# Two products instead of three for every split projection, with ScalarE making the first parts of 30 weights

## The chip, the cores and the metric

The kernel runs on one core of a Trainium2 chip. The metric is the device time of one execution in microseconds (us), lower is better. TensorE multiplies; VectorE, ScalarE and GpSimd work on tiles of 128 partitions; SyncE issues the transfers.

## The reference

Two transformer blocks in float32 on 512 tokens of width 1024 (the second has 16 more tokens of its own, 528 in all), and every matrix product is wanted to float32's accuracy:

```python
# block 1
proj = rms_norm(x, pre_gain) @ w_in              # q, k, v, z_a, b, c, u, z_c
attn = rms_norm(diff_attention(q, k, v)) * silu(z_a)
x = x + rms_norm(concat(attn, conv) @ w_out)     # wo
e = rms_norm(p @ w_ple_proj)
x = x + sigmoid(x @ w_ple_gate) * e              # pg
# block 2
n = rmsnorm(h) @ w_in_2                          # c_q, c_kv, k_pe, gq, gk, gv, gg, gates
y_a = mla_branch(...); y_b = gla_branch(...)
mix = sigmoid(gate_a) * (y_a @ w_o_mla) + sigmoid(gate_b) * (y_b @ w_o_gla)   # ta, oa, tb, ob
h = h + mix @ w_out_2                            # w2
h = h + peer_ffn(rmsnorm(h), w_q, sub_keys, u_tab, v_tab)     # pq, ps, top-k, experts
```

## The kernel before

**Split projections.** A float32 matrix is held as two float32r matrices that TensorE multiplies at its fast rate: a first part, rounded, and the rest. Weights come in groups of 1 MB (128 partitions x 8 x 256 float32), each with a name: q0, k0, v0, q1, ... for block 1, `wo0` to `wo3` for its output projection, `pg0` to `pg3` for its gate; in block 2 cq, ckv, kpe, gq, gk, gv, `ta`, `gg0` to `gg3` (gate of GLA), `tb0` to `tb3` and `ob0` to `ob3` (second gate and output), `w20` to `w23` (output projection), `pq0` to `pq7` (queries of the experts' part, one for each head). `SPLIT` is the list of the split ones in TensorE's order. A weight group is 16 tile products of 512 columns (for the weights that stand as the moving matrix, 32 of 256; in the second block's first projections, 512 tokens and the 16 more go as pieces of 264). `three()` (L799) issues three matmuls for each: first x first (L802), first x rest (L803), rest x first (L804).

**Who makes the parts.** SyncE brings weights into `wring`, NW = 4 slots. On GpSimd `split_group(i)` (L2562) waits for the transfer and, as there are only NU = 2 part buffers, for TensorE's last job with the weights two before (`when_filled(pool, last_job(SPLIT[i - NU]))`), then makes the first part (4 casts of 128x512, L2577) and the rest (4 subtractions, L2581), and signals `weights_split`, for which TensorE waits in `split_arrived` (L792). ScalarE makes first parts of weights only for q0 and k0 (L1516, L1522) and, in `query(h)`, pq6 and pq7 (L1852). For activations, ScalarE rounds (round_gained L1505, round_h L1528, round_pair L1562) and VectorE subtracts (`lower` L2010, L1984, split_pair L2061).

**The stages** in TensorE's order, in us of the profiled execution: block 1's projections and attention 0 to 227; `wo` 227 to 278.5; the gate `pg` to 347.5, whose results pass for each of four m through ScalarE (sigmoid), VectorE (product, sum, gain) and ScalarE (square, rounding); block 2's norm and first projections to 396; MLA's; MLA attention and further projections to 676; GLA to 846; gates and outputs `gg`, `tb`, `ob`, and `w2` to 1028; `pq0`, `pq1` to 1055; the heads' top-k with `pq2` to `pq7` in between to 1137. Then the experts' part: each tile of the table u is multiplied in two products (L1386, L1387) to 1650, and the weighted sum over v (L1438, L1439) to the end. That part already holds its matrices by another rule: with SCALE = 128, GAIN = 127/128, the first part is the rounding of GAIN times the matrix and two products suffice.

**Order.** Each engine works its own list in order; semaphores (`fills`, `empties`, `when_filled`) hand tiles over. In the top-k stretch VectorE picks 16 best for each of 8 heads, GpSimd weighs places (L2613) between its weights, and TensorE scores keys (ps) from `pq`.

## Time and profile before

| | us |
|---|---|
| median of 3 runs | 2176.15 |
| lowest, highest | 2173.21, 2176.32 |
| span of the profiled execution | 2175.9 |
| TensorE busy | 2115.4 (97%) |
| VectorE busy | 1304.1 (60%) |
| GpSimd busy | 1033.5 (47%) |
| ScalarE busy | 922.6 (42%) |

Times of an execution are read from the start of its span. The profiled execution lies within the range of the runs. A row of a timeline gives start, length, engine, line, operation, tiles written and read with shape, how many in a row (x4), and in brackets how long the engine had been idle before it and which instruction ended that. A row of a window gives the stretch, its length, and for each engine its busy time and number of instructions. "PEclk" is the share of full clock that TensorE was granted. Busy times of matmuls overlap, so a row's mean is longer than the distance of two matmuls.

### The profile page before, as it was taken

The page shows a single profiled execution, that of the slowest core. Times are in us where ns is not written, and L with a number is a line of the kernel's source. Part 1 is how long each engine was busy: PE and PEld are TensorE (multiplying, and loading weights), DVE is VectorE, ACT ScalarE, POOL GpSimd, SP SyncE. Part 2 cuts the span into 40 slices and gives each one's busy share as a digit, 9 for nine tenths or more (in the row PEclk, how much of TensorE's full clock was granted, in tenths as well). Part 3 has the DMA queues.
Part 4 walks back from the last instruction along what each step waited for, and adds up shares of the span by engine and source line. Part 5 has one row for each costly group of instructions (what it writes and reads, how often), then busy time and mean ns, then how long its engine had stood idle before and what let it go on. Part 6 is the DMA issues. An engine that isn't in the chain of part 4 may idle for free.

```text
span 2175.9 us, 27394 instructions
## 1 busy us (share of the span) xinstructions
PE 2115.4 (97%) x10296; PEld 1661.6 (76%) x10296; DVE 1304.1 (60%) x2244; ACT 922.6 (42%) x1528; POOL 1033.5 (47%) x892
## 2 busy tenths in 40 slices
PE   8999999999999999999999998999999899999999
PEld 6877767557887776887878877777778788888887
DVE  6456257352235774215898957888881666666664
ACT  4223343572234234111334447777773434343432
POOL 6655546212324122877859887999996100000000
PEclk9999999999999999999999999999999999999999
DMA  5222312201111111233216664777788988888884
GB/s 201 100 78 78 116 61 90 90 30 49 59 40 59 59 55 43 97 122 110 78 59 199 205 206 141 272 289 246 272 291 294 333 300 286 289 284 300 288 287 149
DMA packets 98291, 359.32 MB, mean 165 GB/s; under 512 B 8480, under 2 KB 41504, under 8 KB 73328
## 3 DMA queue, kind: packets, MB, share of 16 engines
q1 hardware_dynamic: 98160, 357.56, 47.3%
q8 instruction: 83, 1.36, 0.3%
q14 instruction: 48, 0.39, 0.1%
HBM read 286.09 MB, written 71.30 MB: 164 GB/s over the span
## 4 chain that ended last, share of the span: by engine, by line
PE 67%; POOL 13%; DVE 11%; issue 6%; ACT 2%; DMA 1%; POOLq 0%; SPq 0%; ACTq 0%; DVEq 0%
PE ps L1438 11%; PE ps L1439 11%; PE ps L802 10%; PE ps L803 9%; PE ps L804 9%; POOL area L2643 6%; POOL wring_parts L2621 6%; PE ps L791 2%; PE ps L1249 2%; DVE area L2413 2%; PE ps L1386 1%; PE ps L1387 1%; DVE area L2410 1%; PE ps L884 1%; PE ps L1225 1%
## 5 line engine op out<-in xcount | busy, mean ns | idle before, releaser
L2577 POOL CAST wring_parts<-wring 128x512 fp32r<-128x512 f32 x236 | 170.5, 764 | 546.0 <-PE ps L804 429.3
L1386 PE MATMUL ps<-sqbuf_parts,wring_parts 128*128 128x512 f32 x1024 | 412.6, 403 | 5.5 <-POOL wring_parts L2621 5.5
L1387 PE MATMUL ps<-normed_x_parts,wring_parts 128*128 128x512 f32 x1024 | 404.4, 395 | 0.0
L2621 POOL TENSOR_TENSOR wring_parts<-wring_parts,wring 128x512 fp32r<-128x512 f32 x256 | 331.0, 1323 | 76.0 <-ACT wring_parts L1856 73.0
L2581 POOL TENSOR_TENSOR wring_parts<-wring,wring_parts 128x512 fp32r<-128x512 f32 x244 | 351.2, 1470 | 6.6 <-ACT wring_parts L1852 1.5
L1386 PEld LDWEIGHTS ps<-sqbuf_parts,wring_parts 128*128 128x128 f32 x1024 | 194.0, 189 | 50.6 <-POOL wring_parts L2621 4.9
L1387 PEld LDWEIGHTS ps<-normed_x_parts,wring_parts 128*128 128x128 f32 x1024 | 193.9, 189 | 41.8
L802 PE MATMUL ps<-resid_parts,wring_parts 128*128 128x512 f32 (+1 forms) x528 | 201.2, 381 | 6.1 <-DVE normed_x_parts L2010 3.3
L803 PE MATMUL ps<-normed_x_parts,wring_parts 128*128 128x512 f32 (+1 forms) x528 | 197.0, 373 | 0.0
L804 PE MATMUL ps<-resid_parts,wring_parts 128*128 128x512 f32 (+1 forms) x528 | 196.2, 372 | 0.0
L1474 ACT ACTIVATE area<-ps 128x1024 f32<-128x1024 f32 (+6 forms) x89 | 61.7, 696 | 275.2 <-PE ps L804 183.5
L2504 DVE COPY area<-ps 128x512 f32<-128x512 f32 x128 | 138.9, 1087 | 56.3 <-PE ps L1413 56.3
L803 PE MATMUL ps<-area_parts,wring_parts 128*128 128x512 f32 x440 | 172.4, 392 | 0.0
L1888 ACT ACTIVATE area<-area,rt 128x128 bf16<-128x128 bf16 x512 | 156.5, 390 | 3.7 <-DVE area L2494 3.7
L1878 ACT ACTIVATE area<-ps 128x512 f32<-128x512 f32 x128 | 76.3, 597 | 187.0 <-PE ps L1387 187.0
L802 PE MATMUL ps<-area_parts,wring_parts 128*128 128x512 f32 x376 | 150.1, 399 | 4.8 <-POOL wring_parts L2581 2.3
L804 PE MATMUL ps<-area_parts,wring_parts 128*128 128x512 f32 x376 | 146.7, 390 | 0.0
L1438 PE MATMUL ps<-cst_parts,area_parts 128*128 128x512 f32 x352 | 138.3, 393 | 4.7 <-issue 4.7
L1439 PE MATMUL ps<-rt_parts,area_parts 128*128 128x512 f32 x352 | 138.0, 392 | 0.0
L1856 ACT ACTIVATE wring_parts<-wring 128x1024 fp32r<-128x1024 f32 x128 | 134.4, 1052 | 7.2 <-DMA wring<-in_uT_dram 7.2
L1438 PE MATMUL ps<-normed_x_parts,area_parts 128*128 128x512 f32 x352 | 136.9, 389 | 0.0
L1439 PE MATMUL ps<-normed_x_parts,area_parts 128*128 128x512 f32 x352 | 136.9, 389 | 0.0
(269 smaller groups left out, 4431.4 us busy)
## 6 DMA issues: line engine op xcount, KB each, us to landing
wring<-in_weights_dram SPq DMA_DIRECT2D x65, 1024.0 KB, 4.8
wring<-in_uT_dram SPq DMA_DIRECT2D x128, 512.0 KB, 4.4
area<-in_vT_dram SPq DMA_DIRECT2D x44, 1024.0 KB, 7.2
hidden_table<-area SPq DMA_DIRECT2D x32, 1024.0 KB, 6.7
gate_table<-area SPq DMA_DIRECT2D x32, 1024.0 KB, 8.4
area<-gate_table SPq DMA_DIRECT2D x32, 1024.0 KB, 9.1
wring<-in_vT_dram SPq DMA_DIRECT2D x20, 1024.0 KB, 6.7
rt<-hidden_table SPq DMA_DIRECT2D x32, 512.0 KB, 4.6
```

The costliest lines, as they stand in the source:

```text
L802: pe.matmul(out, a_up, b_up, start=first, stop=False)
L803: pe.matmul(out, a_up, b_low, start=False, stop=False)
L804: return pe.matmul(out, a_low, b_up, start=False, stop=last)
L1386: pe.matmul(out, first[:, d], h_first[:, k, :], start=(k == 0), stop=False)
L1387: mm = pe.matmul(out, rest[:, d], h_rest[:, k, :], start=False, stop=(k == KD - 1))
L1438: pe.matmul(out, v_first[:, j, d], c_first[:, t], start=(n == 0 and j == 0), stop=False)
L1439: mm = pe.matmul(out, v_rest[:, j, d], c_rest[:, t], start=False, stop=(n == HALVES - 1 and j == 1))
L1888: ins = act.activation(gateB[:, q, i, 0, :], oneB[:, q, i, :], ACT.Copy, scale=entT[:, 2, t:t + 1])
L2504: dve.tensor_copy(dst[:, 4 * i:4 * i + 4, :], spread_out(n)).then_inc(copied, 1)
L2577: ins = nc.gpsimd.tensor_copy(up[:, d, :], W(name)[:, d, :])
L2581: ins = nc.gpsimd.tensor_tensor(low[:, d, :], W(name)[:, d, :], up[:, d, :], ALU.subtract)
L2621: ins = nc.gpsimd.tensor_tensor(rest[:, a:a + PIECE], first[:, a:a + PIECE], u_raw[t % len(USLOT)][:, a:a + PIECE], ALU.subtract)
```

## The change

`three()` becomes `two()`: the first part is now the rounding of GAIN times the weight (or 1/SCALE times the activation), the rest is the first part minus the weight (or 127 times the first part minus the activation), and out = (first x first + rest x rest) comes out 1/128 of the product. The factor 128 is folded into what reads the result. Three gain vectors are multiplied by 128 once at the start, and two additions of VectorE become scalar_tensor_tensor. For 30 weights, listed in `AHEAD_W`, ScalarE makes the first part in two halves of 1024 elements (`round_ahead`), and GpSimd starts its first two subtractions after the first half and the others after the second. All other weights stay on GpSimd, whose cast becomes a multiplication with GAIN.

```diff
+AHEAD_W = ([f"wo{m}" for m in (2, 3)] + [f"pg{m}" for m in range(4)] + ["cq0", "cq1", "gg2", "gg3", "tb0", "ob0", "tb1", "ob1"]
+           + ["tb2", "ob2", "tb3", "ob3"] + [f"w2{m}" for m in range(4)] + [f"pq{m}" for m in range(HP)])
...
-            def three(out, a_parts, b_parts, first, last):
-
-                (a_up, a_low), (b_up, b_low) = a_parts, b_parts
-                pe.matmul(out, a_up, b_up, start=first, stop=False)
-                pe.matmul(out, a_up, b_low, start=False, stop=False)
-                return pe.matmul(out, a_low, b_up, start=False, stop=last)
+            def two(out, a_parts, b_parts, first, last):
+
+                (a_first, a_rest), (b_first, b_rest) = a_parts, b_parts
+                pe.matmul(out, a_first, b_first, start=first, stop=False)
+                return pe.matmul(out, a_rest, b_rest, start=False, stop=last)
...
+            def round_ahead(name):
+
+                i = SPLIT.index(name)
+                up, _ = W_parts(name)
+                act.wait_ge(w_in[WN[name] % NW], 16 * (WN[name] // NW + 1))
+                when_filled(act, last_job(SPLIT[i - NU]))
+                for half in (slice(0, KD // 2), slice(KD // 2, KD)):
+                    act.activation(up[:, half, :], W(name)[:, half, :], ACT.Copy, scale=GAIN).then_inc(ahead_up, 1)
...
             for m in range(4):
                 when_filled(act, ("wo", m))
-                square_two("post", m, pair(("wo", m)))
-                copy_out(("wo", m), mixedT[:, 2 * m:2 * m + 2, :], pair(("wo", m)))
+                round_ahead(("wo2", "wo3", "pg0", "pg1")[m])
+                square_two("post", m, pair(("wo", m)), scale=float(SCALE))
+                copy_out(("wo", m), mixedT[:, 2 * m:2 * m + 2, :], pair(("wo", m)), scale=float(SCALE))
...
             for m in range(4):
-                copy_out(("pg", m), sgT[:, 2 * m:2 * m + 2, :], pair(("pg", m)), ACT.Sigmoid)
+                round_ahead(("pg2", "pg3", "cq0", "cq1")[m])
+                copy_out(("pg", m), sgT[:, 2 * m:2 * m + 2, :], pair(("pg", m)), ACT.Sigmoid, float(SCALE))
...
+            round_ahead("gg2")
             silu(0)
             root("g2", T)
             root("g3", T)
             for h in range(HG):
                 if h + 1 < HG:
+                    round_ahead(("gg3", "tb0", "ob0")[h])
                     silu(h + 1)
                 round_pair(8 + h, O_PARTS, 2 * h, oT)
+            round_ahead("tb1")
             sigmoid(0)
             for m in range(4):
+                round_ahead(("ob1", "ob2", "ob3", "w21")[m])
                 if m + 1 < 4:
+                    round_ahead(("tb2", "tb3", "w20")[m])
                     sigmoid(m + 1)
                 round_pair(12 + m, MIX_PARTS, 2 * m, mixT)
...
             for m in range(4):
+                round_ahead(("w22", "w23", "pq0", "pq1")[m])
                 when_emptied(act, ("w2", m))
...
+            round_ahead("pq2")
+            round_ahead("pq3")
             act.activation(h_first, hs, ACT.Copy, scale=1.0 / SCALE).then_inc(h_rounded, 1)
...
-                if HP - 4 <= h < HP - 2:
-                    name = f"pq{h + 2}"
-                    act.wait_ge(w_in[WN[name] % NW], 16 * (WN[name] // NW + 1))
-                    act.activation(W_parts(name)[0], W(name), ACT.Copy).then_inc(query_up, 1)
+                if 2 <= h < HP - 2:
+                    round_ahead(f"pq{h + 2}")
...
+            for name in ("pre", "mix", "ffn"):
+                at, n = VEC[name]
+                ins = dve.tensor_scalar(vec[:, at:at + n], vec[:, at:at + n], float(SCALE), None, ALU.mult)
+            link(ins)
...
-                    dve.tensor_tensor(h_lower[:, k, 0:width], normed_x[:, k, 0:width], h_upper[:, k, 0:width],
-                                      ALU.subtract).then_inc(h_ready, 1)
+                    dve.scalar_tensor_tensor(h_lower[:, k, 0:width], h_upper[:, k, 0:width], float(SCALE - 1),
+                                             normed_x[:, k, 0:width], ALU.mult, ALU.subtract).then_inc(h_ready, 1)
...
-                if i >= len(SPLIT) - 2:
-                    pool.wait_ge(query_up, i + 3 - len(SPLIT))
-                else:
+                ahead = name in AHEAD_W
+                if not ahead:
                     for d in parts:
-                        ins = nc.gpsimd.tensor_copy(up[:, d, :], W(name)[:, d, :])
+                        ins = nc.gpsimd.tensor_scalar(up[:, d, :], W(name)[:, d, :], GAIN, None, ALU.mult)
                     ins.then_inc(part_rounded, 1)
-                    pool.wait_ge(part_rounded, i + 1)
+                    pool.wait_ge(part_rounded, i + 1 - sum(w in AHEAD_W for w in SPLIT[:i]))
                 for d in parts:
-                    ins = nc.gpsimd.tensor_tensor(low[:, d, :], W(name)[:, d, :], up[:, d, :], ALU.subtract)
+                    if ahead and d.start in (0, k // 2):
+
+                        pool.wait_ge(ahead_up, 2 * AHEAD_W.index(name) + (1 if d.start == 0 else 2))
+                    ins = nc.gpsimd.tensor_tensor(low[:, d, :], up[:, d, :], W(name)[:, d, :], ALU.subtract)
                 ins.then_inc(weights_split, 1)
```

## Rows read from the trace of the kernel before

**Rows 1.** The page of the profile: engines, and GpSimd's cast among the groups.

```profile
PE 2115.4 (97%) x10296; PEld 1661.6 (76%) x10296; DVE 1304.1 (60%) x2244; ACT 922.6 (42%) x1528; POOL 1033.5 (47%) x892
...
L2577 POOL CAST wring_parts<-wring 128x512 fp32r<-128x512 f32 x236 | 170.5, 764 | 546.0 <-PE ps L804 429.3
```

**Rows 2.** Windows of five stretches; the columns stand in the first line.

```profile
core 0: us, PE busy (x) PEld busy (x) DVE busy (x) ACT busy (x) POOL busy (x), PEclk, DMA share, GB/s
40.00:51.60 11.60, 11.60 (x99) 11.46 (x98) 9.89 (x7) 1.93 (x4) 9.26 (x8) 1.00 0.27 92
376.00:381.30 5.30, 5.30 (x31) 5.30 (x32) 1.48 (x3) 0.32 (x1) 0.00 (x0) 0.69 0.02 3
860.40:986.40 126.00, 126.00 (x548) 102.47 (x546) 31.42 (x23) 24.17 (x25) 94.61 (x89) 1.00 0.32 112
988.40:1027.90 39.50, 39.50 (x174) 32.70 (x175) 20.19 (x15) 6.38 (x6) 30.54 (x27) 1.00 0.23 80
1137.30:1304.10 166.80, 165.37 (x704) 133.05 (x705) 138.01 (x550) 71.99 (x92) 150.73 (x104) 0.99 0.61 199
```

**Rows 3.** Windows, line L804 alone: stretch, length, busy (count), clock, DMA share, GB/s.

```profile
0.00:227.00 227.00, 106.16 (x288) 1.00 0.31 110
846.00:1028.00 182.00, 100.08 (x256) 1.00 0.28 99
0.00:1055.00 1055.00, 393.35 (x1096) 0.99 0.23 80
1055.00:1137.00 82.00, 37.38 (x96) 1.00 0.22 76
```

**Rows 4.** Timeline of GpSimd: a weight alone, and a contended first part.

```profile
102.53 2.29 POOL L2577 CAST wring_parts<-wring 128x512 fp32r<-128x512 f32 x4 [4.91 <-PE ps L804]
104.90 5.26 POOL L2581 TENSOR_TENSOR wring_parts<-wring,wring_parts 128x512 fp32r<-128x512 f32 x4
...
872.20 4.27 POOL L2577 CAST wring_parts<-wring 128x512 fp32r<-128x512 f32 x4 [6.64 <-PE ps L804]
```

**Rows 5.** Timeline of ScalarE and VectorE at a pg tile, and a pair's rounding.

```profile
313.52 1.03 ACT L1474 ACTIVATE area<-ps 128x1024 f32<-128x1024 f32 x1 [4.05 <-PE ps L804]
...
314.67 1.22 DVE L2139 TENSOR_TENSOR area<-area 128x1024 f32<-128x1024 f32 x1 [1.09 <-ACT area L1474]
...
317.48 2.15 DVE L1977 TENSOR_SCALAR area<-resid,vec 128x512 f32<-128x512 f32 x2
...
873.02 1.05 ACT L1565 ACTIVATE area_parts<-area 128x1024 fp32r<-128x1024 f32 x1
```

**Rows 6.** Timeline of GpSimd and VectorE, first and second norm.

```profile
31.40 6.72 POOL L2581 TENSOR_TENSOR wring_parts<-wring,wring_parts 128x512 fp32r<-128x512 f32 x4
...
44.72 1.77 DVE L2014 SCALAR_TENSOR_TENSOR normed_x<-resid,vec,rt 128x512 f32<-128x512 f32 x1
46.41 3.48 DVE L2010 TENSOR_TENSOR normed_x_parts<-normed_x,resid_parts 128x512 fp32r<-128x512 f32 x2
...
366.27 0.70 DVE L2010 TENSOR_TENSOR normed_x_parts<-normed_x,resid_parts 128x528 fp32r<-128x528 f32 x1
```

**Rows 7.** Timeline of VectorE, TensorE and ScalarE around waits and roots.

```profile
243.45 1.23 DVE L2061 TENSOR_TENSOR area_parts<-area,area_parts 128x1024 fp32r<-128x1024 f32 x1 [1.13 <-ACT area_parts L1565]
...
375.92 0.59 PE L802 MATMUL ps<-resid_parts,wring_parts 128*128 128x264 f32 x1 [2.76 <-DVE normed_x_parts L2010]
...
859.29 1.28 ACT L1492 ACT_TABLE_LOAD   x1 [0.54 <-PE ps L884]
...
866.53 0.63 ACT L1494 ACTIVATE rt<-rt 128x512 f32<-128x512 f32 x1
...
988.33 0.50 PE L802 MATMUL ps<-area_parts,wring_parts 128*128 128x512 f32 x1 [1.83 <-DVE area_parts L2061]
```

**Rows 8.** Timeline of ScalarE and GpSimd in the top-k stretch.

```profile
1049.81 3.62 ACT L1841 ACTIVATE sqbuf_parts<-normed_x 128x4096 fp32r<-128x4096 f32 x1
...
1108.82 5.68 POOL L2613 TENSOR_TENSOR area<-area 128x1024 f32<-128x1024 f32 x2 [9.32 <-DVE area L2466]
```

More of the change, by code:

```diff
@@ L490, in build @@
         part_rounded = sem("part_rounded")
-        query_up = sem("query_up")
+        ahead_up = sem("ahead_up")
         norm_part = sem("norm_part")
@@ L824, in project_h @@
                             c = (m - tiles[0]) * 512 + at + (MF.start if width == TM else 0)
-                            mm = three(out[:, c:c + n], (up[:, k, d], low[:, k, d]),
+                            mm = two(out[:, c:c + n], (up[:, k, d], low[:, k, d]),
                                        h_parts(k, at, n), k == 0, k == KD - 1)
@@ L838, in project_parts @@
                             pe.wait_ge(pair_split, 4 * turn + n // 2 + 1)
-                        mm = three(pair(key)[:, m, :], (up[:, k, d], low[:, k, d]),
+                        mm = two(pair(key)[:, m, :], (up[:, k, d], low[:, k, d]),
                                    (parts[0][:, k, :], parts[1][:, k, :]), n == 0, n == KD - 1)
@@ L850, in tokens_h @@
                     for k in range(KD):
-                        mm = three(flat(key)[0:n, a * 256:a * 256 + 256], h_parts(k, t * P, n),
+                        mm = two(flat(key)[0:n, a * 256:a * 256 + 256], h_parts(k, t * P, n),
                                    (up[:, k, :], low[:, k, :]), k == 0, k == KD - 1)
@@ L925, in first_query @@
                         d = slice(a * P, (a + 1) * P)
-                        mm = three(pair(key)[:, a, :], (up[:, k, d], low[:, k, d]),
+                        mm = two(pair(key)[:, a, :], (up[:, k, d], low[:, k, d]),
                                    (FIRST_PARTS[0][:, k, :], FIRST_PARTS[1][:, k, :]), k == 0, k == KD - 1)
@@ L938, in first_key @@
                     for k in range(KD):
-                        mm = three(pair(key)[:, a, :], (up[:, k, d], low[:, k, d]),
+                        mm = two(pair(key)[:, a, :], (up[:, k, d], low[:, k, d]),
                                    (FIRST_PARTS[0][:, k, :], FIRST_PARTS[1][:, k, :]), k == 0, k == KD - 1)
@@ L950, in first_value @@
                     for k in range(KD):
-                        mm = three(flat(key)[:, t * 256:t * 256 + 256],
+                        mm = two(flat(key)[:, t * 256:t * 256 + 256],
                                    (FIRST_PARTS[0][:, k, d], FIRST_PARTS[1][:, k, d]), (up[:, k, :], low[:, k, :]),
@@ L1033, in mix_out @@
                         pe.wait_ge(pair_split, {4: 1, 6: 2, 0: 3, 2: 4}[k])
-                    mm = three(pair(key)[:, a, :], (up[:, k, d], low[:, k, d]),
+                    mm = two(pair(key)[:, a, :], (up[:, k, d], low[:, k, d]),
                                (MIXIN_PARTS[0][:, k, :], MIXIN_PARTS[1][:, k, :]), k == 4, k == 3)
@@ L1074, in latent_query @@
                             d = slice(a * P, (a + 1) * P)
-                            mm = three(pair(key)[:, a, :], (up[:, k, d], low[:, k, d]),
+                            mm = two(pair(key)[:, a, :], (up[:, k, d], low[:, k, d]),
                                        (X2_PARTS[0][:, k, :], X2_PARTS[1][:, k, :]), k == 0, k == KD - 1)
@@ L1236, in gate_quarter @@
                 for k in range(4 * (q % 2), 4 * (q % 2) + 4):
-                    mm = three(pair(key)[:, m, :], (up[:, k, d], low[:, k, d]), h_parts(k, 0, T), k == 0, k == KD - 1)
+                    mm = two(pair(key)[:, m, :], (up[:, k, d], low[:, k, d]), h_parts(k, 0, T), k == 0, k == KD - 1)
                 if q == 3:
@@ L1350, in raw_query @@
                             d = slice(a * P, (a + 1) * P)
-                            mm = three(pair(key)[:, a, :], (up[:, k, d], low[:, k, d]),
+                            mm = two(pair(key)[:, a, :], (up[:, k, d], low[:, k, d]),
                                        (X3_PARTS[0][:, k, :], X3_PARTS[1][:, k, :]), k == 0, k == KD - 1)
@@ L1564, in round_pair @@
                 act.wait_ge(pair_made, n + 1)
-                act.activation(parts[0][:, k:k + 2, :], src[:, k:k + 2, :], ACT.Copy).then_inc(pair_rounded, 1)
+                act.activation(parts[0][:, k:k + 2, :], src[:, k:k + 2, :], ACT.Copy, scale=1.0 / SCALE
+                               ).then_inc(pair_rounded, 1)
             def copy_a(h):
@@ L1983, in split_gained @@
                 x = slice(2 * m, 2 * m + 2)
-                dve.tensor_tensor(parts[1][:, x, :], src[:, x, :], parts[0][:, x, :], ALU.subtract
-                                  ).then_inc(gained_low, 1)
+                dve.scalar_tensor_tensor(parts[1][:, x, :], parts[0][:, x, :], float(SCALE - 1), src[:, x, :],
+                                         ALU.mult, ALU.subtract).then_inc(gained_low, 1)
             for m in range(4):
@@ L2060, in split_pair @@
                 dve.wait_ge(pair_rounded, n + 1)
-                dve.tensor_tensor(parts[1][:, k:k + 2, :], src[:, k:k + 2, :], parts[0][:, k:k + 2, :],
-                                  ALU.subtract).then_inc(pair_split, 1)
+                dve.scalar_tensor_tensor(parts[1][:, k:k + 2, :], parts[0][:, k:k + 2, :], float(SCALE - 1),
+                                         src[:, k:k + 2, :], ALU.mult, ALU.subtract).then_inc(pair_split, 1)
             def conv_part(m):
@@ L2368, in _ @@
                     dve.wait_ge(pair_made, 12 + m)
-                empties(dve.tensor_tensor(mix_tmp, gate_s[:, m % 2, :, :], pair(("ob", m)), ALU.mult), ("ob", m))
+                empties(dve.scalar_tensor_tensor(mix_tmp, pair(("ob", m)), float(SCALE), gate_s[:, m % 2, :, :],
+                                                 ALU.mult, ALU.mult), ("ob", m))
                 when_emptied(dve, ("ob", m))
@@ L2378, in _ @@
                 x = resid[:, 2 * m:2 * m + 2, 0:T]
-                empties(dve.tensor_tensor(x, x, pair(("w2", m)), ALU.add), ("w2", m))
+                empties(dve.scalar_tensor_tensor(x, pair(("w2", m)), float(SCALE), x, ALU.mult, ALU.add), ("w2", m))
                 when_emptied(dve, ("w2", m))
@@ L2596, in lower_first @@
                         pool.wait_ge(w_in[WN[name]], 16)
-                    ins = nc.gpsimd.tensor_tensor(low[:, k, :], W(name)[:, k, :], up[:, k, :], ALU.subtract)
+                    ins = nc.gpsimd.tensor_tensor(low[:, k, :], up[:, k, :], W(name)[:, k, :], ALU.subtract)
                     if i == 0 and m < 3:
```

17 lines of the change are left out of this document (9 added, 8 removed).

## The prediction

> **What bounds the kernel now.** The page first: TensorE is busy 97% of the span, GpSimd 47% [rows 1]. But a share over the whole span mixes stages, so I cut it with the windows view. In 860.40 to 986.40 TensorE has no idle time and issues 548 matmuls in 126.00 us, 0.230 each; in 1137.30 to 1304.10, where each weight tile serves two products, 704 take 0.237; the 256-column products of v0 cost 11.60 / 96 = 0.121 [rows 2]. So a product costs its columns, one of 264 by that 0.125 at most. In the same windows GpSimd works 94.61 of 126.00 us [rows 2]. Next the windows of the line of the third product: 1096 of them before 1055 us, 288 of these before 227 and 256 in 846 to 1028, then 96 [rows 3]. Last, the timelines of GpSimd, ScalarE and VectorE at the hand-offs [rows 4 to 8].
>
> **The ceiling.** Before 1055 us, 1096 third products go: 760 of 512 columns, 112 of 264, 224 of 256 (by the code). 760 × 0.230 + 112 × 0.125 + 224 × 0.121 = 216 us. The 96 of pq2 to pq7 (22 us) lie in the top-k stretch: there VectorE's choice of the best 16 of a head is what all wait for: GpSimd waits 9.32 us for VectorE before it can weigh places and go on to pq7 [rows 8]; I count them at nothing.
>
> **What is late next.** A weight now asks 32 products, 7.4 us (before 48, 11.0). Two part buffers: part i may start at F(i−2), the end of the product that used its buffer. GpSimd alone took 2.29 + 5.26 = 7.55 us; with VectorE beside it 4.27 [rows 4] + 6.72 [rows 6] = 11.0 at worst. Alone that no longer keeps up with 7.4, hence ScalarE's halves: 1.05 us each [rows 5], GpSimd's four subtractions start after the first. The hand-off is then L = 1.05 + 5.3 to 6.7 + some 0.2 = 6.5 to 8.0. With two buffers the period is (L + 7.4)/2 where L is over 7.4, nothing is lost below.
>
> SyncE's transfers of weights run four slots ahead and a slot comes free sooner than before; the DMA share is 0.32 in the densest projection stretch [rows 2] and would be 0.32 × 11 / 7.4 = 0.48: no new wait.
>
> The unseen operation is GpSimd's multiply in place of the cast (weights not in the list). Its bounds: the cast's 2.29 / 4 = 0.57 us a piece and the two-input subtraction's 5.26 / 4 = 1.32 [rows 4]; 3.0 us a weight between them. It has one input, as the cast: I take 0.57. VectorE's scalar_tensor_tensor for subtract: L2014, one, and L2010, the subtraction on the same tile, take 1.77 and 3.48 / 2 = 1.74 [rows 6]: nothing. Folded scales are in operations that are there; three multiplies of gain vectors (128 x 8 each) at the start come while VectorE waits for x: nothing; uncovered they would be under 1 us.
>
> **Stage by stage** (ceiling, then what I keep of it).
>
> *Start and attention, 0 to 227: 59.3 (224 × 0.230 + 64 × 0.121), keep 51.7.* q1 needs the normed x, whose last part ends at 49.89 [rows 6]; v0 ends at 51.6 now. With q0, k0, v0 shorter by 11.2 that norm is what q1 waits for: its first pass can't end before 49.9, the second takes 3.7, so it ends at 54 where now 62.6 (51.6 + 48 × 0.230). Of 14.9 to there (11.2 + 3.7), 8.9 remain, 6.0 lost. GpSimd makes v0 and q1 in at most 11.0 us each, v0 from q0's end against 7.4 of k0: hidden behind the same norm. Later the first scores wait for their head's probabilities, which ScalarE and VectorE make no sooner: 1.6 more, my estimate.
>
> *wo, 227 to 278.5: 14.7, keep 9.6.* wo0 needs the mix-in split ending at 244.68 [rows 7], a chain that does not shorten, so half of wo0's 3.7 is lost: 1.9. wo2 may be begun only at wo0's end, and with 1.05, GpSimd's 6.7 and ScalarE's and the queues' delays L is 8.2 to 9.2 against 7.4: 1.8 by the upper end; a clock fall after that gap, 1.4. That price is a row: after a 2.76 us gap TensorE ran at 0.69 granted clock (between the levels 1.2 and 2.4 GHz) in 376 to 381.3, 14 matmuls at 0.22 us pitch, not 0.12 [rows 2, 7]: 14 × 0.1 = 1.4. After a gap of 1.83 us it did not fall (1.00 in 988.4 to 1027.9) [rows 2, 7].
>
> *pg and the second norm, 278.5 to 396: 26.4, keep 12.* pg0 keeps 3.3. pg1 to pg3 hand over to a loop of ScalarE and VectorE: copy 1.03, VectorE's two (317.48 − 314.67 = 2.8) and 2.15, ScalarE's square and rounding (1.05), and the two new halves (2.1) in ScalarE's order ahead of the copy [rows 5]: 1.03 + 2.8 + 2.15 + 1.05 + 2.1 = 9.1, with semaphores 9.3, not 7.4. Against 11.0 that is 1.7 × 3 = 5.4 with rounding. The 24 wide products before the norm are covered by it: 0. After the norm 6.1 less 1.4 (clock) and 1.4 (GpSimd's 7.6 to 11.0 for weights not in the list): 3.3.
>
> *MLA attention, 491 to 676: 34.9, keep 32.7.* gv0 stays on GpSimd, 7.6 to 11.0 (I take 8.8) against 7.7 for the weight before: 1.1 lost, and as much at two other hand-offs.
>
> *GLA, 676 to 846: 14.7, keep 14.2.* Its weights stand far apart, with TensorE's other work as cover; 0.5 for one hand-off.
>
> *Gates, outputs, w2, 846 to 1028: 58.9, keep 46.8.* Lost: 3.5 at gg3, whose rounding stands in ScalarE's order behind the roots of g2 and g3, which with four table loads take (866.53 + 0.63) − 859.29 = 7.9 us [rows 7]. From gg0's end ScalarE has 2.1 (gg2's halves) + 1.9 (silu, copy 1.03 [rows 5] and a multiply) + 7.9 = 11.9, then 1.05 + 5.3 make gg3 ready at 18.3, when TensorE is through gg1 and gg2 at 14.8. The rest: 1.3 at w20, where TensorE comes sooner to VectorE's split of the mix, so that the 1.83 us wait becomes 3.1 [rows 7]; ob1 to ob3, w21 and their partners have L of 8.3 to 8.8 (ScalarE busy with sigmoids and pairs when asked): 3.0 together; w22 to pq1 1.5; two clock falls 2.8. Sum 12.1.
>
> *pq0, pq1, 1028 to 1055: 7.4, keep 1.0.* ScalarE rounds pq2 and pq3, 4 × 1.05 = 4.2 us, before its 3.62 us of h_first and the copy of ps0 [rows 8], from which VectorE's first head starts; 2.2 more, my estimate, as pq2 is asked later. That chain, not TensorE, is followed from there.
>
> Sum: 51.7 + 9.6 + 12 + 32.7 + 14.2 + 46.8 + 1.0 = 168.0. The page's execution has a span of 2175.9; the median of the runs is 2176.15. From the span: **2008 us**.
>
> A rule that speaks against the change: the Trainium skill, SBUF — State Buffer, section "SBUF: two separate sides", says that GpSimd and a two-input VectorE operation hold one port pair by turns, the loser blocked for the whole instruction. The trace agrees where both are busy (cast 4.27 for 2.29 [rows 4], L2010 3.48 / 2 = 1.74 for 0.70 [rows 6]). By it the shorter stretches make VectorE's work denser and L would be its upper 8 us everywhere instead of 6.5 to 8: some 25 weights × 0.3 = 8 us more. The Trainium skill, GPSIMD Engine Reference, section "Performance versus the Vector engine", gives one-input bodies with up to two operations the port's rate, which would make the multiply cost what the cast does.
>
> **Rivals.**
>
> *All hand-offs hidden (0.13).* GpSimd waits 429 us for TensorE at the cast [rows 1], so there is slack; ScalarE is busy 42% [rows 1]. If L is 6.5 everywhere and no clock falls, wo's 3.2, the 2.8 behind the norm, MLA's 2.2, GLA's 0.5, the gates' 12.1 and the scores' 1.6 come back, 22.4: 1986. Against it: the cast's contended row.
>
> *GpSimd's multiply is dear, or ScalarE's halves late (0.20).* At the upper bound +3.0 us for a weight made by GpSimd alone: v0, q1 and some seven more bind, 9 × 2 to 3 = 18 to 27: 2026 to 2035. Late halves in the gate stretch (each stands near a silu or sigmoid of 1.03 [rows 5], with a table load of 1.28 [rows 7]) would cost 16 × 0.8 = 13: 2021.
>
> *The clock ends it on the other side (0.02).* Two products before 1055 take 1520 × 0.230 + 224 × 0.125 + 448 × 0.121 = 432 us at 1.00. If the waits brought the low level, at half speed, they cost up to 432 more, less the idle gaps that they fill, some 354 (0.82 of it: TensorE's share in 0 to 1055 that is behind no other wait, my estimate). It decides from the point where 168 / 354 = 47% of that time is low. For it: 0.69 after one gap. Against: 0.99 and 1.00 in the two long windows [rows 2].
>
> *The third product was no bound (0.01 for no change, 0.02 for a gain of 30 to 100 us).* If stages were carried by VectorE, the gain would shrink to those with PE full; against it, 0.230 × 548 = 126.00 us without an idle moment [rows 2].
>
> **From these the numbers.** The forecast (within 1992 to 2020) has 0.62; hidden 0.13; dear or late 0.20; low clock 0.02; weak gain 0.03. The range leaves out the lowest part of the second and the farthest of the third: 1988 to 2036. Under 0.2% (4.4 us) is about what this kernel's runs can't tell from nothing (the three before lie within 0.14%). Faster 0.97, same 0.01, slower 0.02.
>
> **What would show it.** Right: no third product; 0.230 us each still; q1 ends near 54; a period near 9.3 in the pg loop; a gap of 3 to 4 us ahead of gg3; pieces of GpSimd's multiply near 0.6 to 0.8; the first u tile near 1137 − 168 = 969; from there to the end the same 1039 us. Wrong: multiply pieces near 1.3; TensorE waiting for GpSimd's subtraction at most weights by over 1 us; granted clock below 0.9 in a whole stretch; or the stretch behind the first u tile longer, since transfers start otherwise.

## The result and the profile after

The changed kernel takes 2047.34 us (median of 4 runs, 2043.4 to 2051.2) against 2176.24 for the kernel before: a ratio of 0.9403, with a 95% interval of 0.9383 to 0.9423. That is 129 us faster. The forecast was 168 us faster (2008), in a range of 1988 to 2036: the direction was right, the time lies outside. The profiled execution has a span of 2043.6 us.

The page of the changed kernel: engines, the line of the granted clock, and groups.

```profile
PE 1908.6 (93%) x9104; PEld 1481.9 (73%) x9104; DVE 1292.5 (63%) x2247; ACT 974.6 (48%) x1586; POOL 1060.3 (52%) x782
...
PEclk9999997999999999999899999999999999999999
...
L2611 POOL TENSOR_TENSOR wring_parts<-wring_parts,wring 128x512 fp32r<-128x512 f32 x244 | 352.2, 1475 | 137.9 <-ACT wring_parts L1522 135.0
...
L2604 POOL TENSOR_SCALAR wring_parts<-wring 128x512 fp32r<-128x512 f32 x126 | 197.5, 1591 | 247.0 <-PE ps L808 153.8
...
L807 PE MATMUL ps<-resid_parts,wring_parts 128*128 128x512 f32 (+1 forms) x528 | 203.5, 393 | 25.5 <-POOL wring_parts L2611 16.1
```

The third product is gone (9104 matmuls, before 10296 [rows 1]), and TensorE's share fell from 97% to 93%. What is new is the second GpSimd group: the multiplication (L2604) takes 1591 ns a piece, where the cast took 764 [rows 1], and the idle time ahead of it that ends with TensorE is 153.8 us, before 429.3 (with 126 pieces, before 236). The clock has a digit 7 and an 8 in its line. The single pieces (shortest, median and longest in ns) show that the multiplication is dear at its shortest too:

```profile
L2604 POOL TENSOR_SCALAR wring_parts<-wring x126: 1484/1493/2397, 26.4 to 734.5; 128x512 fp32r<-128x512 f32 x126
```

Windows of the changed kernel: attention, wo and ple, the end of pg with the norm, the gate stretch, the top-k stretch. Columns as in [rows 2].

```profile
core 0: us, PE busy (x) PEld busy (x) DVE busy (x) ACT busy (x) POOL busy (x), PEclk, DMA share, GB/s
52.00:201.00 149.00, 132.28 (x580) 99.85 (x578) 83.16 (x131) 54.48 (x109) 147.92 (x105) 0.94 0.30 105
201.00:266.00 65.00, 58.25 (x188) 37.30 (x189) 21.37 (x20) 35.45 (x37) 33.32 (x24) 0.95 0.31 108
307.00:352.00 45.00, 32.84 (x151) 26.61 (x151) 27.45 (x30) 19.83 (x27) 22.61 (x14) 0.77 0.27 86
762.00:913.00 151.00, 138.61 (x565) 108.04 (x564) 76.61 (x56) 80.01 (x82) 99.63 (x64) 0.97 0.38 132
913.00:1000.00 87.00, 66.64 (x335) 56.44 (x334) 79.44 (x348) 30.55 (x30) 45.38 (x28) 0.88 0.21 72
```

From 52 to 201 us GpSimd is busy 147.92 of 149.00 us. That is the finding of the whole case: in attention GpSimd, not TensorE, sets the pace (experiments 1, 2, 3 and 6 test it). The timeline of GpSimd shows one weight after another there, none of them with idle time in brackets:

```profile
94.99 5.92 POOL L2604 TENSOR_SCALAR wring_parts<-wring 128x512 fp32r<-128x512 f32 x4
100.99 5.12 POOL L2611 TENSOR_TENSOR wring_parts<-wring_parts,wring 128x512 fp32r<-128x512 f32 x4
106.07 6.16 POOL L2604 TENSOR_SCALAR wring_parts<-wring 128x512 fp32r<-128x512 f32 x4
```

Four multiplications 5.92 us, four subtractions 5.12: 11.1 us a weight, against TensorE's 7.4 for the weight's products. Uncontended cast and subtractions had taken 7.55 [rows 4]. TensorE's waits, its two largest groups (columns: line, released by, us in all, times, longest; the 13.2 are pq7's, in the stretch that VectorE paces):

```profile
engine line waited for: us in total, times, longest us
PE ps L807 <- POOL wring_parts L2611: 54.7, 19, 13.2
PE ps L1416 <- POOL area L2673: 13.3, 27, 2.7
```

The same products in the two traces, found by count of tile products, give what each stage gained. A time in this table, and every start of a weight further down, is the start of the last product of the stage's or weight's first tile (the third product before, the second after). Beside it stand the forecast and a run that comes below (GpSimd casts and doesn't multiply).

| stage (first tile to first tile) | forecast | changed kernel | with the cast |
|---|---|---|---|
| start and attention, to wo0 (230.7 before; 201.2; 177.4) | 51.7 | 29.5 | 53.3 |
| wo and ple, to pg0 | 9.6 | 6.6 | 7.3 |
| pg and the norm, to gq | 12 | 9.8 | 7.5 |
| MLA and its attention, to ta0 | 32.7 | 26.7 | 32.7 |
| GLA, to gg0 | 14.2 | 15.2 | 13.0 |
| gates, outputs, w2, to pq0 | 46.8 | 44.0 | 43.6 |
| pq0 to VectorE's first head | 1.0 | −1.4 | −1.3 |
| first head to the end | 0 | +1.9 | −2.3 |
| sum | 168.0 | 132.3 | 153.8 |

Of the 35.7 us that are missing, 22.2 are in the first stage and 6.0 in MLA's, both with weights that GpSimd makes alone.

### The profile page after: what moved, and what is told of

It is laid out like the page before. It is cut to its first block, busy times and chain, and to the rows that moved or that the text cites. A ratio compares the mean times of both kernels' runs of the same rounds, so it can differ in the third digit from the quotient of the medians.

```text
span 2043.6 us, 24990 instructions
## 1 busy us (share of the span) xinstructions
PE 1908.6 (93%) x9104; PEld 1481.9 (73%) x9104; DVE 1292.5 (63%) x2247; ACT 974.6 (48%) x1586; POOL 1060.3 (52%) x782
## 4 chain that ended last, share of the span: by engine, by line
PE 49%; POOL 24%; DVE 14%; issue 7%; ACT 5%; DMA 1%; POOLq 0%; SPq 0%; ACTq 0%; DVEq 0%
PE ps L1442 11%; PE ps L1443 11%; POOL area L2673 6%; POOL wring_parts L2651 6%; POOL wring_parts L2611 6%; POOL wring_parts L2604 5%; PE ps L807 5%; PE ps L808 5%; PE ps L1253 3%; PE ps L796 3%; DVE area L2441 2%; PE ps L1390 2%; PE ps L1391 2%; DVE area L2438 2%; DVE area L2469 1%
## 5 line engine op out<-in xcount | busy, mean ns | idle before, releaser
L2611 POOL TENSOR_TENSOR wring_parts<-wring_parts,wring 128x512 fp32r<-128x512 f32 x244 | 352.2, 1475 | 137.9 <-ACT wring_parts L1522 135.0
L2651 POOL TENSOR_TENSOR wring_parts<-wring_parts,wring 128x512 fp32r<-128x512 f32 x256 | 328.6, 1315 | 71.2 <-ACT wring_parts L1879 67.4
L2604 POOL TENSOR_SCALAR wring_parts<-wring 128x512 fp32r<-128x512 f32 x126 | 197.5, 1591 | 247.0 <-PE ps L808 153.8
L807 PE MATMUL ps<-resid_parts,wring_parts 128*128 128x512 f32 (+1 forms) x528 | 203.5, 393 | 25.5 <-POOL wring_parts L2611 16.1
L807 PE MATMUL ps<-area_parts,wring_parts 128*128 128x512 f32 x376 | 157.1, 418 | 35.7 <-POOL wring_parts L2611 21.8
L808 PE MATMUL ps<-area_parts,wring_parts 128*128 128x512 f32 x440 | 178.3, 405 | 0.0
L807 PEld LDWEIGHTS ps<-resid_parts,wring_parts 128*128 128x128 f32 x528 | 103.9, 197 | 52.1 <-issue 27.1
L2673 POOL TENSOR_TENSOR area<-area,rt 128x512 bf16<-128x512 bf16 x128 | 130.9, 1044 | 1.7 <-DVE area L2522 1.5
```

What stands on the lines that cost most here:

```text
L807: pe.matmul(out, a_first, b_first, start=first, stop=False)
L808: return pe.matmul(out, a_rest, b_rest, start=False, stop=last)
L2604: ins = nc.gpsimd.tensor_scalar(up[:, d, :], W(name)[:, d, :], GAIN, None, ALU.mult)
L2611: ins = nc.gpsimd.tensor_tensor(low[:, d, :], up[:, d, :], W(name)[:, d, :], ALU.subtract)
L2651: ins = nc.gpsimd.tensor_tensor(rest[:, a:a + PIECE], first[:, a:a + PIECE], u_raw[t % len(USLOT)][:, a:a + PIECE], ALU.subtract)
L2673: nc.gpsimd.tensor_tensor(gateB[:, n % 4, :, 1, :], oneB[:, n % 4], w, ALU.mult).then_inc(gates_low, 1)
```

## The experiments

Each kernel is the changed one with the edit shown. "Starts" of weights are read as in the table above. Ratios are to the kernel before, with the 95% interval in brackets; the changed kernel's is 0.9403 (0.9383 to 0.9423). One thousandth is 2.2 us.

**1. GpSimd casts again.**

```diff
-    ins = nc.gpsimd.tensor_scalar(up[:, d, :], W(name)[:, d, :], GAIN, None, ALU.mult)
+    ins = nc.gpsimd.tensor_copy(up[:, d, :], W(name)[:, d, :])
```

> GpSimd makes its first parts with the cast of the kernel before in place of the multiplication with 127/128; this leaves that factor out of these weights, all else as in the changed kernel. Theory 1 (the multiplication sets the pace: in the trace after, a piece takes 1.485 us at the least, where the cast took 0.57, and GpSimd is busy 147.92 of the 149 us from 52 to 201): a weight costs GpSimd about 7.6 to 8.5 us, not 11.1, wo0 starts some 20 to 25 us sooner, and the run is at 2005 to 2020 us. Rival (the loss sits in ScalarE's late halves or in the clock): under 8 us of change, 2040 us or more.

Measured: 2019.07 us, ratio 0.926 (0.9242 to 0.9278), 31 us less than the changed kernel by the ratios. The group of the cast, the window of attention and GpSimd's timeline in it:

```profile
L2611 POOL TENSOR_TENSOR wring_parts<-wring_parts,wring 128x512 fp32r<-128x512 f32 x244 | 361.6, 1513 | 151.9 <-ACT wring_parts L1522 149.1
...
L2604 POOL CAST wring_parts<-wring 128x512 fp32r<-128x512 f32 x126 | 87.8, 738 | 307.8 <-PE ps L808 203.6
```

```profile
52.00:177.00 125.00, 119.31 (x554) 89.31 (x554) 94.21 (x125) 50.72 (x99) 104.72 (x103) 1.00 0.34 117
```

```profile
101.23 2.29 POOL L2604 CAST wring_parts<-wring 128x512 fp32r<-128x512 f32 x4 [1.15 <-PE ps L808]
103.60 5.67 POOL L2611 TENSOR_TENSOR wring_parts<-wring_parts,wring 128x512 fp32r<-128x512 f32 x4
109.58 2.29 POOL L2604 CAST wring_parts<-wring 128x512 fp32r<-128x512 f32 x4 [0.30 <-PE ps L808]
```

The piece is 738 ns where the multiplication took 1591, GpSimd has idle time in brackets again (1.15, 0.30), released by TensorE, and is busy 104.72 of 125 us. wo0 starts at 177.4, 23.8 us sooner, and the first stage keeps 53.3 us, MLA's 32.7. So the loss in these two stages is the price of this one operation. In the traces the first u tile comes 25.4 us sooner (977.4, not 1002.8). The rival (under 8 us) falls.

**2. GpSimd multiplies by a column.** The same product, as a tensor_tensor with a column that holds 127/128 (set once), broadcast over the piece.

```diff
+nc.gpsimd.memset(small[:, 316:317], GAIN).then_inc(gain_set, 1)
...
-    ins = nc.gpsimd.tensor_scalar(up[:, d, :], W(name)[:, d, :], GAIN, None, ALU.mult)
+    ins = nc.gpsimd.tensor_tensor(up[:, d, :], W(name)[:, d, :], small[:, 316:317].unsqueeze(2)
+                                  .to_broadcast([P, d.stop - d.start, n]), ALU.mult)
```

> GpSimd multiplies by a column that holds 127/128, with a tensor_tensor operation, in place of the tensor_scalar with a number. Theory 1 (the price of a piece goes one for one into the 13 weights of attention and the few others): if a piece takes 1.32 us as the subtraction does, 4 x 0.165 = 0.66 us a weight, 8 to 12 us faster than the changed kernel; if the broadcast column makes it dearer than 1.485, slower by 4 us for each 0.1 us of a piece. Rival (GpSimd's time a weight does not set the pace): within 2 us.

Measured: 2035.89 us, ratio 0.9346 (0.9325 to 0.9367), 12 us less. The group of the multiplication, and its single pieces (shortest, median, longest in ns):

```profile
L2607 POOL TENSOR_TENSOR wring_parts<-wring,small 128x512 fp32r<-128x512 f32 x126 | 149.3, 1214 | 272.2 <-PE ps L809 176.6 <-DMA wring<-in_weights_dram 95.5
...
L2607 POOL TENSOR_TENSOR wring_parts<-wring,small x126: 1034/1042/2032, 25.5 to 719.9; 128x512 fp32r<-128x512 f32 x126
```

A piece takes 1214 ns in the mean (1.03 us at the least), less than the number's 1591 and, uncontended, less than the subtraction's 1.26 to 1.32, which reads two full tiles. So three prices of the first part, 0.57 (the cast's 2.29 / 4), 1.03 and 1.485 us uncontended, give three times, 2019, 2036 and 2047: the time follows the price. It doesn't follow one for one, as had been expected: 0.45 us × 4 × 13 weights would be 23 us, and 12 are saved (wo0 starts at 193.0, 8.2 us sooner).

**3. A third product put back.**

```diff
     pe.matmul(out, a_first, b_first, start=first, stop=False)
+    pe.matmul(out, a_rest, b_first, start=False, stop=False)
```

> The changed kernel with a third product put back (rest x first, a spare one; the output then holds one term too many). Theory 1 (with 11.0 us of TensorE a weight the 11.1 to 12.5 us of GpSimd are nearly hidden): 2180 to 2195 us, and TensorE is nearly never idle in the gate stretch. Rival (GpSimd's multiplication costs as much here as with two products): 2205 us or more.

Measured: 2181.28 us, ratio 1.0004 (0.9994 to 1.0015). GpSimd's timeline in attention:

```profile
119.86 5.96 POOL L2605 TENSOR_SCALAR wring_parts<-wring 128x512 fp32r<-128x512 f32 x4 [3.39 <-PE ps L809]
125.90 5.03 POOL L2612 TENSOR_TENSOR wring_parts<-wring_parts,wring 128x512 fp32r<-128x512 f32 x4
132.49 2.95 POOL L2605 TENSOR_SCALAR wring_parts<-wring 128x512 fp32r<-128x512 f32 x2 [1.56 <-PE ps L809]
```

The multiplication costs the same 5.96 us for four, but GpSimd has waits of 3.39 and 1.56 us for TensorE: with 11.0 us a weight on TensorE, GpSimd's 11.1 are covered, and this kernel takes the time of the kernel before to 0.1%. In the kernel before, the third product had left room for such a price; the change takes that room away.

**4. GpSimd makes all first parts.** ScalarE's 30 weights go back to GpSimd.

```diff
-AHEAD_W = ([f"wo{m}" for m in (2, 3)] + ...
+AHEAD_W = ()
...
 def round_ahead(name):
+    if name not in AHEAD_W:
+        return
```

> Two products, but GpSimd makes the first parts of the 30 weights too. Theory 1 (GpSimd needs 11.2 us alone and up to 13 beside VectorE, and TensorE 7.4): each of some 24 weights in the stretches without attention costs 3.5 to 5 us more, 85 to 115 us in all: 2130 to 2160 us. Rival (TensorE waits for other engines in these stretches, and the halves hide nothing): under 30 us slower, up to 2077 us.

Measured: 2111.04 us, ratio 0.9694 (0.9673 to 0.9715), 63 us slower than the changed kernel, between the two expectations. Its multiplications:

```profile
L2607 POOL TENSOR_SCALAR wring_parts<-wring 128x512 fp32r<-128x512 f32 x244 | 390.3, 1623 | 286.2 <-PE ps L809 193.6 <-DMA wring<-in_weights_dram 92.6
```

The stretches after attention lose it, from gg0 to pq0 44.5 us (768.3 to 953.0 where the changed kernel has 758.9 to 899.1), and 13 more between pq0 and the u tiles (1069.3), where the queries' weights are GpSimd's too. The halves on ScalarE are worth 63 us, less than the 85 to 115 expected. From wo0 to gq only 9.4 us are lost (201.1 to 462.2, where the changed kernel has 201.2 to 452.9), though eight of the 30 weights lie there; which engine covers them was not looked into.

**5. Whole roundings.** One operation of 2048 elements for each of the 30 weights.

```diff
-    for half in (slice(0, KD // 2), slice(KD // 2, KD)):
-        act.activation(up[:, half, :], W(name)[:, half, :], ACT.Copy, scale=GAIN).then_inc(ahead_up, 1)
+    act.activation(up, W(name), ACT.Copy, scale=GAIN).then_inc(ahead_up, 2)
```

> The 30 weights are rounded in one operation each, not in halves. Theory 1 (where GpSimd waits for ScalarE's half, the hand-off of a weight is 0.9 us longer, and the period half of it): 20 weights x 0.45 us, 6 to 12 us slower than the changed kernel. Rival (GpSimd is late by its own queue, and the half hides nothing): within 2 us.

Measured: 2055.95 us, ratio 0.9436 (0.9415 to 0.9457), 7 us slower by the ratios (11.5 by the spans, 2055.1 and 2043.6). The intervals of the two ratios overlap, so this rests on the starts too: pq0 comes at 908.2, 9.1 us later. The hand-off's length counts, at about the size expected (6 to 12).

**6. ScalarE in attention too.**

```diff
-AHEAD_W = ([f"wo{m}" for m in (2, 3)] + ...
+AHEAD_W = (SPLIT[5:18] + [f"wo{m}" for m in (2, 3)] + ...
...
     if u + 2 < len(UNITS_A):
         exps_a(u + 2)
+    if u in SIDE_A:
+        round_ahead(SPLIT[5 + list(SIDE_A).index(u)])
```

> ScalarE also makes in halves the first parts of v1, c0 to za1, wo0 and wo1, each behind the exponentials of a unit of attention; v0, q1 and k1 stay on GpSimd. Theory 1 (GpSimd's multiplication is what bounds 60 to 201): GpSimd is left with 5 to 7 us a weight, the stretch to wo0 shortens by 20 to 35 us, and the run is at 2012 to 2027 us. Rival (ScalarE's 2.1 us a unit push exponentials and copies back and TensorE waits for these): less than 10 us faster, or slower.

Measured: 2028.9 us, ratio 0.9312 (0.9296 to 0.9328), 20 us less than the changed kernel and 2 us above the range expected. The window of attention:

```profile
52.00:180.00 128.00, 124.14 (x576) 93.32 (x575) 83.94 (x129) 75.06 (x128) 74.11 (x55) 1.00 0.34 117
```

GpSimd is busy 74.11 of 128 us, TensorE 124.14, at a clock of 1.00 (before this edit 0.94): wo0 starts at 180.0. From q1 to wo0 it takes 129.5 us, with the cast 131.1: ScalarE's 2 us a unit were hidden.

**7. gg3 between the roots.** The largest wait of the gate stretch, in the trace of the changed kernel: TensorE ahead of gg3, and ScalarE's last operations before gg3's rounding.

```profile
790.42 0.77 PE L807 MATMUL ps<-resid_parts,wring_parts 128*128 128x512 f32 x1 [5.95 <-POOL wring_parts L2611]
790.98 0.63 PE L808 MATMUL ps<-normed_x_parts,wring_parts 128*128 128x512 f32 x1
791.41 0.63 PE L807 MATMUL ps<-resid_parts,wring_parts 128*128 128x512 f32 x1
```

```profile
777.12 1.28 ACT L1496 ACT_TABLE_LOAD   x1
...
780.41 0.63 ACT L1498 ACTIVATE rt<-rt 128x512 f32<-128x512 f32 x1
780.95 1.99 ACT L1522 ACTIVATE wring_parts<-wring 128x1024 fp32r<-128x1024 f32 x2
```

The rounding comes at 780.95, straight behind the roots; TensorE stands 5.95 us and then has a distance of 0.43 us between products.

```diff
     root("g2", T)
+    round_ahead("gg3")
     root("g3", T)
     for h in range(HG):
         if h + 1 < HG:
-            round_ahead(("gg3", "tb0", "ob0")[h])
+            if h:
+                round_ahead(("gg3", "tb0", "ob0")[h])
```

> ScalarE rounds gg3 between the roots of g2 and g3, not behind both. In the trace after, TensorE waits 5.95 us ahead of gg3 and then runs 13 products at the low clock. Theory 1 (the order of ScalarE makes this wait): the roots of g3 no longer stand ahead of the rounding, the wait falls to 0 to 2 us, no clock fall follows, and the run is 5 to 8 us faster than the changed kernel. Rival (GpSimd is late with gg2 or gg3 for its own reasons): under 2 us.

Measured: 2038.54 us, ratio 0.9357 (0.9335 to 0.9379), 10 us less by the ratios and 6.2 by the spans; pq0 starts 4.4 us sooner (894.7). The rounding and TensorE's next wait:

```profile
777.58 2.01 ACT L1522 ACTIVATE wring_parts<-wring 128x1024 fp32r<-128x1024 f32 x2
```

```profile
795.66 0.47 PE L807 MATMUL ps<-resid_parts,wring_parts 128*128 128x512 f32 x1 [3.40 <-POOL wring_parts L2613]
```

The wait ahead of gg3 is gone, but tb0, later in ScalarE's order behind the roots of g3, now has one of 3.40, and the clock falls there instead (0.66 from 795 to 800 us). The order of ScalarE was a cause, and a part of the wait moved on. It was not the only one: in the changed kernel GpSimd's four subtractions of gg3 took 8.11 us, beside VectorE, where the sum had 5.3:

```profile
782.17 8.11 POOL L2611 TENSOR_TENSOR wring_parts<-wring_parts,wring 128x512 fp32r<-128x512 f32 x4 [6.89 <-ACT wring_parts L1522]
```

**8. Spare products in the waits.** TensorE multiplies tiles whose results are overwritten, while it waits. The call stands in three such places; one is shown.

```diff
+FILL = {"wo1": 16, "wo2": 8, "pg3": 12, "gg3": 22}
+def keep_busy(name, out, moving):
+    for _ in range(FILL.get(name, 0)):
+        pe.matmul(out, moving[:, 0:P], moving, start=True, stop=True)
...
     claim(key)
+    keep_busy(name, flat(key)[:, 0:T], h_upper[:, 0, 0:T])
```

> TensorE multiplies 16, 8, 12 and 22 spare tiles, whose results are overwritten, while it waits ahead of wo1, wo2, pg3 and gg3 (waits of 4.4, 2.3, 3.6 and 5.95 us in the trace after). Theory 2 (part of the gap to the forecast is the clock: some 100 products of projections run at 0.43 us, not 0.23, right after waits): at these four places the products run at 0.23 us, and the run is 3 to 7 us faster than the changed kernel. Rival (the low clock falls into time that a later wait takes anyway): no low clock there, and within 2 us of the changed kernel.

Measured: 2043.99 us, ratio 0.9387 (0.9364 to 0.9409); pq0 starts at 894.2, 4.9 us sooner, of which 1.1 is there at wo0 already, ahead of the first spare product. Windows around the four places, first of the changed kernel, then of this one:

```profile
200.00:240.00 40.00, 32.32 (x122) 25.02 (x123) 8.96 (x6) 18.45 (x19) 26.92 (x20) 0.91 0.37 131
285.00:300.00 15.00, 11.40 (x43) 8.91 (x42) 10.78 (x10) 9.09 (x10) 9.66 (x7) 0.89 0.33 105
785.00:800.00 15.00, 9.58 (x30) 7.65 (x31) 8.26 (x4) 4.97 (x6) 12.19 (x7) 0.77 0.21 72
```

```profile
200.00:240.00 40.00, 38.28 (x159) 29.46 (x159) 9.09 (x6) 18.05 (x19) 27.93 (x20) 1.00 0.33 121
285.00:300.00 15.00, 14.17 (x61) 10.91 (x60) 11.97 (x9) 5.85 (x7) 12.11 (x8) 1.00 0.33 107
780.00:800.00 20.00, 19.09 (x83) 15.29 (x82) 11.95 (x7) 11.38 (x12) 17.95 (x11) 1.00 0.30 105
```

The clock was 0.91, 0.89 and 0.77, and is 1.00 at all of them. In the changed kernel some 80 products of 512 columns run at a distance of about 0.43 us in place of 0.23, in ten places, 4 to 12 at a time, and some 90 of 256 or 264 columns at about 0.22 in place of 0.12, in five places; most of these places are behind a wait of 2 us or more. That is some 25 us more than at full clock; before it was under 2. (Counted from the starts of consecutive products in the trace; not all of it sets the end.) The forecast had four such falls of 1.4 us. The total's interval overlaps that of the changed kernel, so the gain of some 4 us rests on the trace's starts.

**9. Late queries.** 

```diff
-    round_ahead("pq2")
-    round_ahead("pq3")
     act.activation(h_first, hs, ACT.Copy, scale=1.0 / SCALE).then_inc(h_rounded, 1)
...
     copy_out(("ps", h), sc[:, h].rearrange("p a b -> p (a b)"), flat(("ps", h)))
+    if h == 0:
+        round_ahead("pq2")
+        round_ahead("pq3")
```

> ScalarE rounds pq2 and pq3 after h_first and the copy of ps0, not ahead of them. Theory 1 (from VectorE's first head on, VectorE alone sets the pace up to the u tiles, so the 3.9 us of roundings ahead of the copy are lost one for one): the first head starts 3.5 to 4 us sooner and the run is 3 to 4 us faster than the changed kernel. Rival (pq2 comes later by as much, or the head waits for other things): within 1 us of the changed kernel.

Measured: 2045.08 us, ratio 0.9382 (0.9359 to 0.9405). ScalarE and VectorE's first head, in the changed kernel and then in this one:

```profile
917.49 3.88 ACT L1522 ACTIVATE wring_parts<-wring 128x1024 fp32r<-128x1024 f32 x4
921.28 3.61 ACT L1866 ACTIVATE sqbuf_parts<-normed_x 128x4096 fp32r<-128x4096 f32 x1
924.79 1.00 ACT L1478 ACTIVATE area<-ps 128x1024 f32<-128x1024 f32 x1
```

```profile
925.82 1.65 DVE L2438 MAX8 area<-area 128x8 f32<-128x128 f32 x8 [5.85 <-ACT area L1478]
```

```profile
918.13 3.60 ACT L1864 ACTIVATE sqbuf_parts<-normed_x 128x4096 fp32r<-128x4096 f32 x1
921.64 1.01 ACT L1478 ACTIVATE area<-ps 128x1024 f32<-128x1024 f32 x1
922.54 3.88 ACT L1522 ACTIVATE wring_parts<-wring 128x1024 fp32r<-128x1024 f32 x4
```

```profile
922.68 1.65 DVE L2439 MAX8 area<-area 128x8 f32<-128x128 f32 x8 [2.06 <-ACT area L1478]
```

The roundings (3.88 us) stood ahead of h_first and the copy, as forecast; now the head starts at 922.68, not 925.82, and the u tiles at 1000.1, not 1002.8. Counted from pq0 (899.8 here, 899.1 there) the head comes 3.8 us sooner. The total doesn't tell it from no change: the span is 2043.8 against 2043.6, since the stretch behind the first u tile, which no edit touches, took 1043.7 us here and 1040.8 there. Inconclusive in the time, shown in the stretch.

**10. Cast, order and spare products together.** Edits 1 and 7, and spare products ahead of wo1 (12), wo2 (7), pg3 (12) and tb0 (10). Like 1, it leaves the factor 127/128 out of GpSimd's first parts.

> Three edits at once, to see whether they close the way to the forecast: GpSimd's cast in place of the multiplication (leaves the factor 127/128 out of these weights), gg3 rounded between the roots of g2 and g3, and spare products of TensorE ahead of wo1 (12), wo2 (7), pg3 (12) and tb0 (10). Theory 1 with theory 2 (multiplication 28 us, order of ScalarE 4 to 5, clock 3 to 5): 2047 less 36 to 38, so 2008 to 2013 us, about the forecast. Rival (the edits fall into each other's waits): 2015 us or more.

Measured: 2011.75 us, ratio 0.9227 (0.9197 to 0.9257), which on the kernel before's 2176.24 is 2008. The first u tile comes at 964.9 (forecast 969). The edits add up, as expected (2008 to 2013). That the total meets the forecast is in part luck: edit 7 and the spare products take away waits and low clock that the forecast had counted as lost (3.5 us at gg3, 5.6 for the clock).

**11 and 12. A faster version.** Edits 2, 6, 7 and 9, and then the spare products of 10 as well.

> A version meant to be faster than both: ScalarE also rounds v1 to wo1 in halves, GpSimd multiplies what is left by a column (1.04 us a piece, not 1.49), gg3 is rounded between the roots, pq2 and pq3 behind the copy of ps0. Theory 1 (attention 20 us, the column some 3 more for the weights left, gg3 4.5, the queries 2 to 4): 2013 to 2020 us. Rival (ScalarE is now the bound in attention): 2022 us or more.

Measured: 2022.45 us, ratio 0.9288 (0.9271 to 0.9304). This misses the 2013 to 2020 expected and lies where the rival had it, but the trace doesn't bear the rival's cause out: from 52 to 180 us ScalarE is busy 74.29 of 128.00 us and TensorE 123.01. Why the edits give less together than the sum expected was not looked into.

> The version with ScalarE's halves in attention too, the column, gg3 between the roots and the late queries, with TensorE's spare products ahead of wo1 (12), wo2 (7), pg3 (12) and tb0 (10). Theory 2 (each fall of the clock costs 1.4 to 2.6 us where TensorE sets the pace): three or four falls less, 3 to 7 us faster than the same without spare products, a ratio near 0.926. Rival (the low clock lies in time that later waits take): ratio within 0.001 of 0.9288.

Measured: 2017.55 us, ratio 0.9269 (0.9256 to 0.9281), 1.4% under the changed kernel; both compute all that the changed kernel does. The spare products give 4 us by the ratios, and the intervals overlap; pq0 starts 4.3 us sooner (871.3, 875.6), and wo0 at nearly the same time (181.5, 181.6), so the starts show the gain. The ratio lies between the two expectations, nearer to 0.926. Edit 2 added nothing to 6 in attention, where few weights are left to GpSimd (wo0 at 181.6, not 180.0).

## Why the prediction was wrong

**The step that failed** is "It has one input, as the cast: I take 0.57", and the bounds beside it. GpSimd's multiplication by a number takes 1.485 us uncontended and 1.59 in the mean. That lies even above the bound that I had taken from the two-input subtraction (1.32). The nearest row was chosen by the number of inputs, and by it the cast; the run with the column, two inputs and 1.03 us, shows that the number of inputs doesn't order these prices. The Trainium skill (GPSIMD Engine Reference, "Performance versus the Vector engine") gives a one-input body of one or two operations the port's rate, about one cycle an element. By its 1.2 GHz that is an estimate of 0.44 us for 512 elements. The cast comes near it with 0.57; the multiplication does not, and the measurement decides. Restoring the cast gives back 23.8 us to wo0; in all it gives 25.4 us at the first u tile, 28 by the medians and 31 by the ratios, of the 36 to 39 missing.

**The rival had the mechanism, and nearly its price.** "GpSimd's multiply is dear" had 0.20, 18 to 27 us and so 2026 to 2035. The price was 25 to 31 us. It came about otherwise than the rival said (3.0 us more a weight for nine weights). A weight costs 3.5 us more alone (11.1 for 7.55), and GpSimd is never idle from 26.4 to 212.7 us, over all 16 weights from v0 to wo1, so one weight's lateness passes to the next. Much of the price is still hidden, as TensorE has scores and transposes between the weights: from q1 to wo0, 13 weights, it comes to 18.5 us (149.6 for 131.1 with the cast), 1.4 a weight, and 5.3 more lie before q1. In MLA's stage the whole 6.0 us lie at one weight, gv0, for which TensorE waits 4.47 us (the forecast had 1.1 lost there). The others there are covered; GpSimd itself waits for TensorE before most of them:

```profile
540.28 6.04 POOL L2604 TENSOR_SCALAR wring_parts<-wring 128x512 fp32r<-128x512 f32 x4 [18.48 <-PE ps L808]
```

A range that reached to 2036 on this rival was too narrow for two reasons. Its end was a row of another operation, and it set the rival's price on top of an otherwise exact 2008; the run with the cast stands at 2019 (2015 by its ratio), so 7 to 11 us were missing besides.

**What stood.** The ceiling and TensorE's prices stood: 0.23 us a product. With the cast, attention keeps 53.3 us for 51.7 and MLA 32.7 for 32.7, and q1's last product starts at 53.2, where the forecast had its end at 54 (58.6 with the multiplication). GLA gave 15.2 for 14.2. From the first head on VectorE sets the pace, as said; the roundings ahead of it cost 3.1 us (3.8 from pq0), for the 4.2 counted.

**Near by luck: the gate stretch's sum** (44.0 for 46.8). Two terms in it were wrong and partly cancel. TensorE waits 5.95 us ahead of gg3, where 3.5 was forecast, and then runs 12 products at the low clock. ScalarE's part of that term held (12.1 us from gg2's halves at 768.82 to gg3's at 780.95, for 11.9); what was mis-sized is GpSimd's four subtractions, 8.11 us for the 5.3 taken, above the contended 6.7 too. On the other side, the 3.0 us for ob1 to ob3, w21 and their partners were not lost: from ob0 to w20 the weights' starts stand 7.3 to 7.7 us apart, TensorE's own time. The wait ahead of w20 was right, 3.23 for 3.1. In the mean the subtractions did not become dearer (L2611 1475 ns; L2581 before 1470).

**Mis-sized: the clock.** 5.6 us were counted; some 25 us of stretched products are in the trace, of which by the runs with spare products some 4 count at the four places. The low clock cost some us and did not turn the sign. One of the forecast's own signs of being wrong, a granted clock below 0.9 in a whole stretch, came true for 307 to 352 us (0.77) and 913 to 1000 (0.88).

**Right for ScalarE's halves:** they are worth 63 us, and a longer hand-off costs time where ScalarE rounds (experiments 4 and 5).

**Left open.** That pg and the norm keep 7.5 us with the cast and 9.8 without may in part be the clock. The step from pg0's to the second block's first product is alike in both (40.5 us); behind it, from 378 to 430 us, the run with the cast has a granted clock of 0.93, where the changed kernel has 0.97 from 400 to 452, in both behind waits for VectorE. No run tests it. The stretch behind the first u tile takes 1038.6 us before, 1040.8 after, and 1044.7 and 1047.3 in experiments 1 and 10, though its instructions are the same. It doesn't go with the size of the gain: 1038.6 in experiment 7, 1046.6 with the third product put back. No run looked into it; it puts some us into every total that no edit accounts for.

## What to carry to other kernels

When a change takes work from the engine that sets the pace, price the replaced operations of the engine behind it as if they were the bound, because they become it. An operation that no trace shows has no bound from its neighbour's row: give it a range that the neighbours don't close, and try the other ways to write it (a number, a column, a cast), which here stand at 1.485, 1.03 and 0.57 us. Before a weight is given to a helper engine only in some stages, look at whether that engine has room in the others too: 20 us lay there.
